# Two norms summed less their shift with one root operation, and softmax shares divided on ScalarE

## The reference, cut to what matters

```python
def layer_norm(x, g, b):
    mu = jnp.mean(x, -1, keepdims=True)
    var = jnp.mean(jnp.square(x - mu), -1, keepdims=True)
    return (x - mu) * lax.rsqrt(var + LN_EPS) * g + b

h = layer_norm(concatenate([meta, x]), emb_ln_g, emb_ln_b)        # "mean_e" in the kernel
for i in range(2):
    u = h @ w_in[i]                       # q, k, v, convolution input, two gates
    y_attn = sliding_window_attention(...) @ w_attn_proj[i]       # softmax with a sink
    y_conv = conformer_conv(...) @ w_conv_proj[i]                 # 31 taps, norm, silu
    mix = (sigmoid(ga) * y_attn + sigmoid(gc) * y_conv) @ w_out[i]
    h = layer_norm(ALPHA * h + mix, ln1_g[i], ln1_b[i])           # "n10", "n11"
    f = swiglu(h, ...) if i == 0 else moe_swiglu(h, ...)
    h = layer_norm(ALPHA * h + f, ln2_g[i], ln2_b[i])             # "n2", then the last norm

def sink_softmax(s, sink):
    m = jnp.maximum(jnp.max(s, -1, keepdims=True), sink)
    p = jnp.exp(s - m)
    return p / (jnp.sum(p, -1, keepdims=True) + jnp.exp(sink - m))
```

## Time and profile before

| what | value |
|---|---|
| median of 3 executions | 1641.17 us (1640.95 to 1641.51) |
| the profiled execution's own time | 1641.93 us |
| its span | 1640.1 us |
| PE busy | 1614.9 us, 98% of the span |
| PE's weight loads busy | 1472.9 us, 90% |
| DVE busy | 1240.9 us, 76% |
| ACT busy | 968.3 us, 59% |
| POOL busy | 304.4 us, 19% |
| mean granted TensorE clock, as a share of full speed | 0.999 |

### The profile page before, as it was taken

The page is one execution under the profiler, slowest core; times in us unless marked ns, Lnnn a source line. Parts: engine busy times, 40 slices in busy tenths (PEclk is TensorE's granted clock), DMA queues, the critical chain, the costliest instruction groups (busy, mean ns, idle before and its releaser), DMA issues.

```text
span 1640.1 us, 27535 instructions
## 1 busy us (share of the span) xinstructions
PE 1614.9 (98%) x11024; PEld 1472.9 (90%) x11024; DVE 1240.9 (76%) x1770; ACT 968.3 (59%) x1379; POOL 304.4 (19%) x301
## 2 busy tenths in 40 slices
PE   9999999999999999999999999999999999999997
PEld 8988888898888889989999999999988888888886
DVE  6565776666567656998975545899988898998897
ACT  6556674346657634555554433555568677776775
POOL 1230652123236302052300002131210000000000
PEclk9999999999999999999999999999999999999999
DMA  9732555563245546432435554534439898988983
GB/s 336 254 121 86 180 189 189 187 230 131 103 180 183 202 163 227 154 142 103 167 142 180 180 180 172 180 129 151 159 132 339 328 346 342 338 336 331 353 339 125
DMA packets 50740, 340.78 MB, mean 208 GB/s; under 512 B 5611, under 2 KB 7819, under 8 KB 11184
## 3 DMA queue, kind: packets, MB, share of 16 engines
q1 hardware_dynamic: 47920, 329.83, 54.9%
q0 software_dynamic: 2544, 9.12, 1.8%
q10 hardware_dynamic: 144, 0.01, 0.0%
HBM read 337.81 MB, written 1.13 MB: 207 GB/s over the span
## 4 chain that ended last, share of the span: by engine, by line
PE 86%; DVE 4%; issue 3%; ACT 3%; POOL 2%; DMA 1%; SPq 0%; POOLq 0%; DVEq 0%; ACTq 0%
PE bank L564 12%; PE bank L538 8%; PE bank L540 8%; PE bank L539 8%; PE bank L562 7%; PE bank L994 5%; PE bank L995 5%; PE bank L996 5%; PE bank L1027 2%; PE bank L1026 2%; PE bank L1025 2%; PE bank L691 2%; PE bank L693 2%; PE bank L692 2%; PE bank L444 1%
## 5 line engine op out<-in xcount | busy, mean ns | idle before, releaser
L1745 DVE TENSOR_TENSOR wl<-stg,wh 128x2048 fp32r<-128x2048 f32 x308 | 708.0, 2302 | 206.9 <-ACT wh L1239 204.2
L1239 ACT ACTIVATE wh<-stg 128x2048 fp32r<-128x2048 f32 x308 | 588.9, 1912 | 181.0 <-PE bank L996 81.3
L538 PE MATMUL bank<-xx,wh 128*128 128x272 f32 (+1 forms) x778 | 225.3, 290 | 0.0
L540 PE MATMUL bank<-xx,wl 128*128 128x272 f32 (+1 forms) x778 | 223.1, 287 | 0.0
L539 PE MATMUL bank<-xx,wh 128*128 128x272 f32 (+1 forms) x778 | 223.0, 287 | 0.0
L564 PE MATMUL bank<-xx,wh 128*128 128x512 f32 x448 | 159.7, 396 | 0.0
L564 PE MATMUL bank<-H,wh 128*128 128x512 f32 x434 | 151.3, 390 | 0.0
L994 PE MATMUL bank<-wh,GH 128*128 128x512 f32 (+3 forms) x400 | 147.5, 369 | 0.0
L539 PEld LDWEIGHTS bank<-xx,wh 128*128 128x128 f32 x778 | 147.4, 190 | 0.0
L538 PEld LDWEIGHTS bank<-xx,wh 128*128 128x128 f32 x778 | 146.4, 188 | 1.1 <-issue 0.7
L540 PEld LDWEIGHTS bank<-xx,wl 128*128 128x128 f32 x778 | 146.3, 188 | 0.0
(11 more groups left out here) (385 smaller groups left out, 3545.1 us busy)
## 6 DMA issues: line engine op xcount, KB each, us to landing
stg<-in_w SPq DMA_DIRECT2D x308, 1024.0 KB, 4.9
BT<-bias_scratch POOLq DMA_DIRECT2D x3, 1024.0 KB, 9.7
stg<-in_first SPq DMA_DIRECT2D x4, 512.0 KB, 6.1
stg<-in_w SPq DMA_DIRECT2D x4, 512.0 KB, 9.4
BT<-bias_scratch POOLq DMA_DIRECT2D x1, 2048.0 KB, 12.0
BB<-bias_scratch POOLq DMA_DIRECT2D x2, 1024.0 KB, 6.6
res<-in_x SPq DMA_DIRECT2D x1, 1024.0 KB, 8.8
BB<-bias_scratch POOLq DMA_DIRECT2D x2, 512.0 KB, 7.2
```

Source lines behind the costliest of these rows:

```text
L538: pe.matmul(out, wh, xh(kt), start=kt == 0, stop=False)
L540: ins = pe.matmul(out, wl, xh(kt), start=False, stop=kt == KT - 1)
L1239: act.activation(WH[u % NW][:, :], stg[place(u)][:, :], ACT.Copy).then_inc(*m.inc("w_high", u))
L1745: vec.tensor_tensor(WL[u % NW][:, :], stg[place(u)][:, :], WH[u % NW][:, :].bitcast(F32), ALU.subtract).then_inc(*m.inc("w_low_v", u))
```

## The change

Two things are changed. For the norms mean_e and n2 the sums, the root and the order of the last part get new forms (`..._ahead`); n10 and n11 keep theirs. In both mixing layers the shares move from POOL's program into ACT's.

- ACT makes 7 and 8 times the shift (`XC[3]` with a negative sign, `XC[5]`); POOL adds the former to the running sum.
- One tile ahead, DVE makes the last tile's known part less the shift (`less_shift`, `XC[6]`) and the first tile less the shift (`XC[2]`). At the last tile DVE first adds the product's part to it (`last_tile`), ahead of the sum into `RES`; PE and ACT take it from there.
- PE sums "less" (three terms less the shift), then the variance, then a plain mean, and then 4 instead of 11 products of ones.
- ACT squares the mean less shift and takes one Abs_reciprocal_sqrt where Ln and Exp were; its table is loaded at the place where the other's was.
- DVE makes the variance in one operation; the order over the tiles becomes normed, the low part of the tile before, the next centring.

```diff
+AHEAD_OF_SUMS = ("mean_e", "n2")
+            def last_sums_ahead(stage, name):
+                pe.matmul(PS[b][:, 0:T], ones, RS, start=True, stop=False)
+                pe.matmul(PS[v][:, 0:T], ones, SQ[:, 0, 0:T], start=True, stop=False)
+                w.wait_ge(*m.of("last_tile", name))
+                pe.matmul(PS[b][:, 0:T], ones, XC[:, KD - 2, :], start=False, stop=True)   # "less"
+                w.wait_ge(*m.of("shifted_sq", (name, KD - 1)))
+                pe.matmul(PS[v][:, 0:T], ones, SQ[:, KD - 1, 0:T], start=False, stop=True) # "var"
+                pe.matmul(PS[f][:, 0:T], ones, RS, start=True, stop=False)
+                pe.matmul(PS[f][:, 0:T], ones, XC[:, KD - 3, :], start=False, stop=False)
+                pe.matmul(PS[f][:, 0:T], ones, XC[:, KD - 2, :], start=False, stop=True)   # "mean"
+                keep_warm(4)
...
             def mix_layer(l, st):                                          # PE
-                        w.wait_ge(*m.of("shares", (tag, t)))
+                        w.wait_ge(*m.of("mixed_shares", (tag, t)))
...
+            def shifted_ahead(name, nt):                                   # ACT, last tile
+                    act.preload_act_table_set(ROOT)
+                    w.wait_ge(*m.of("last_tile", name))
+                    act.activation(SQ[:, KD - 1, :], XC[:, KD - 2, :], ACT.Square, scale=D ** -0.5)
+            def guess_ahead(name):
+                w.wait_ge(*m.of("group", (name, "less")))
+                act.activation(BC[:, :], bank((name, "less"))[:, 0:T], ACT.Square, scale=1.0 / D)
+                w.wait_ge(*m.of("var_out", name))
+                act.activation(BC[:, :], SQ[:, 2, :], ACT.Abs_reciprocal_sqrt)
+                sp.one_ahead()
...
                 def step(i):                                               # ACT, mixing layers
+                    d = i - 2
+                    if 0 <= d < len(jobs):
+                        L = a["L"][d % DEEP][0:nq, 1:1 + jobs[d]["nk"]]
+                        w.wait_ge(*m.of("recip", (tag, d)))
+                        act.activation(L, L, ACT.Copy, scale=a["z"][0:nq, d % (DEEP + 2), 4:5])
                     t = i - DEEP
...
+            def less_shift(name, scale):                                   # DVE
+                    ins = vec.tensor_tensor(XC[:, KD - 2, :], RES[:, KD - 1, :], SH, ALU.subtract)
+                vec.tensor_tensor(XC[:, 2, :], RES[:, 0, :], SH, ALU.subtract)
+            def last_tile(name, part, lo):
+                vec.tensor_tensor(XC[:, KD - 2, lo:T], XC[:, KD - 2, lo:T], part, ALU.add)
+            def shifted_norm_ahead(name, gname, l, low):
+                vec.scalar_tensor_tensor(v, var, LN_EPS, BC[:, :], ALU.add, ALU.subtract)  # var_out
+                first_tile()
+                w.wait_ge(*m.of("guess", name))
...
+                for kt in range(KD + 1):
+                    if kt < KD:
+                        w.wait_ge(*m.of("centred", (name, kt)))
+                        vec.scalar_tensor_tensor(SQ[:, kt, :], XC[:, kt if kt else 2, :], ...) # normed
+                    if kt == 0:
+                        w.wait_ge(*m.of("group", (name, "mean")))
+                        centre(1)
+                    if kt > 0:
+                        low(kt - 1)
+                    if 0 < kt < KD - 1:
+                        centre(kt + 1)
...
             def mix_layer(l):                                              # POOL
-                        w.wait_ge(*m.of("recip", (tag, i)))
-                        pool.tensor_scalar(L, L, z[0:j["nq"], 4:5], None, ALU.mult)
```

More of the change, by code:

```diff
@@ L773, in pump @@
                     if nt == 2:
-                        b, old = bank((name, "shift"), ("shift", name))
+                        b, old = bank((name, "shift"), ("shift_7" if name in AHEAD_OF_SUMS else "shift", name))
                         vacant(old)
@@ L798, in last_sums @@
                 keep_warm(11)
+            def last_sums_ahead(stage, name):
+                b, old = bank((name, "less"), ("centred", (name, 0)))
+                vacant(old)
+                w.wait_ge(*m.of("res_added", (name, "shifted")))
+                pe.matmul(PS[b][:, 0:T], ones, RS, start=True, stop=False)
+                v, old = bank((name, "var"), ("var_out", name))
+                vacant(old)
+                w.wait_ge(*m.of("sq_added", (name, KD - 2)))
+                pe.matmul(PS[v][:, 0:T], ones, SQ[:, 0, 0:T], start=True, stop=False)
+                w.wait_ge(*m.of("last_tile", name))
+                pe.matmul(PS[b][:, 0:T], ones, XC[:, KD - 2, :], start=False, stop=True).then_inc(*m.inc("group", (name, "less")))
+                w.wait_ge(*m.of("shifted_sq", (name, KD - 1)))
+                pe.matmul(PS[v][:, 0:T], ones, SQ[:, KD - 1, 0:T], start=False, stop=True).then_inc(*m.inc("group", (name, "var")))
+                f, old = bank((name, "mean"), ("centred", (name, KD - 1)))
+                if name == "n11":
+                    held.add(f)
+                vacant(old)
+                w.wait_ge(*m.of("shift_8", name))
+                pe.matmul(PS[f][:, 0:T], ones, RS, start=True, stop=False)
+                pe.matmul(PS[f][:, 0:T], ones, XC[:, KD - 3, :], start=False, stop=False)
+                pe.matmul(PS[f][:, 0:T], ones, XC[:, KD - 2, :], start=False, stop=True).then_inc(*m.inc("group", (name, "mean")))
+                keep_warm(4)
+            def last_sums(stage, name):
+                (last_sums_ahead if name in AHEAD_OF_SUMS else last_sums_plain)(stage, name)
             def mix_layer(l, st):
@@ L1431, in guess @@
                 sp.one_ahead()
+            def guess_ahead(name):
+                w.wait_ge(*m.of("group", (name, "less")))
+                act.activation(BC[:, :], bank((name, "less"))[:, 0:T], ACT.Square, scale=1.0 / D).then_inc(*m.inc("mean_sq", name))
+                w.wait_ge(*m.of("var_out", name))
+                act.activation(BC[:, :], SQ[:, 2, :], ACT.Abs_reciprocal_sqrt).then_inc(*m.inc("guess", name))
+                sp.one_ahead()
+            def guess(name):
+                (guess_ahead if name in AHEAD_OF_SUMS else guess_plain)(name)
             def split_norm(name, bname, l):
@@ L1475, in step @@
                 def step(i):
+                    d = i - 2
+                    if 0 <= d < len(jobs):
+                        nq = jobs[d]["nq"]
+                        L = a["L"][d % DEEP][0:nq, 1:1 + jobs[d]["nk"]]
+                        w.wait_ge(*m.of("recip", (tag, d)))
+                        act.activation(L, L, ACT.Copy, scale=a["z"][0:nq, d % (DEEP + 2), 4:5]).then_inc(*m.inc("mixed_shares", (tag, d)))
                     t = i - DEEP
@@ L1970, in shifted, with shifted_ahead, shifted_norm_plain @@
                     sp.hold()
-            def shifted_norm(name, gname, l, low):
+            def shifted_ahead(name, nt):
+                if nt == 3:
+                    w.wait_ge(*m.of("shift", name))
+                if nt == KD - 1:
+                    return
+                for kt in SHIFTED.get(nt, ()):
+                    w.wait_ge(*m.last("res"))
+                    vec.tensor_tensor(SQ[:, kt, :], RES[:, kt, :], SH, ALU.subtract).then_inc(*m.inc("shifted", (name, kt)))
+                if name == "n11" and nt == KD - 3:
+                    sp.hold()
+            def shifted(name, nt):
+                (shifted_ahead if name in AHEAD_OF_SUMS else shifted_plain)(name, nt)
+            def less_shift(name, scale):
+                if scale is None:
+                    ins = vec.tensor_tensor(XC[:, KD - 2, :], RES[:, KD - 1, :], SH, ALU.subtract)
+                else:
+                    ins = vec.scalar_tensor_tensor(XC[:, KD - 2, :], RES[:, KD - 1, :], scale, SH, ALU.mult, ALU.subtract)
+                ins.then_inc(*m.inc("less_shift", name))
+                vec.tensor_tensor(XC[:, 2, :], RES[:, 0, :], SH, ALU.subtract).then_inc(*m.inc("first_less", name))
+            def last_tile(name, part, lo):
+                w.wait_ge(*m.of("less_shift", name))
+                vec.tensor_tensor(XC[:, KD - 2, lo:T], XC[:, KD - 2, lo:T], part, ALU.add).then_inc(*m.inc("last_tile", name))
+            def shifted_norm_plain(name, gname, l, low):
                 d, v, t = SQ[:, 1, :], SQ[:, 2, :], SQ[:, 3, :]
@@ L2008, in shifted_norm, with centre, first_tile @@
                         low(kt - 1)
+            def shifted_norm_ahead(name, gname, l, low):
+                v, t = SQ[:, 2, :], SQ[:, 3, :]
+                less, mean, var = (bank((name, part))[:, 0:T] for part in ("less", "mean", "var"))
+                def centre(kt):
+                    vec.scalar_tensor_tensor(XC[:, kt, :], mean, -1.0 / D, RES[:, kt, 0:T], ALU.mult, ALU.add).then_inc(*m.inc("centred", (name, kt)))
+                def first_tile():
+                    w.wait_ge(*m.of("first_less", name))
+                    vec.scalar_tensor_tensor(XC[:, 2, :], less, -1.0 / D, XC[:, 2, :], ALU.mult, ALU.add).then_inc(*m.inc("centred", (name, 0)))
```

(33 more changed lines are left out.)

35 lines of the change are left out of this document (28 added, 7 removed).

## The result

The changed kernel took 1647.23 us (median of 7 runs, 1645.97 to 1648.38), the kernel before 1641.16 (7 runs, 1640.95 to 1641.51): a ratio of 1.0037, interval [1.0028, 1.0047]. The forecast was 1641.8 with a range to 1644.6; the time lies above it. The profiled execution took 1648.38 with a span of 1646.6.

The account below looks back on a forecast made before the run. The prediction took PE, 86% of the chain, as the bound, with DVE pacing the mixing layers. Its terms, -0.45 (mean_e, layer 0) and +1.1 (n2, layer 1), summed to +0.65: 1641.8 us, range 1637.7 to 1644.6.

Parts of the forecast that it names:

- the shares' price: Mixing layers: each share holds ACT's queue 0.42 or 0.32, delaying later work; priced at each layer's first values product.
- -0.45 for mean_e with layer 0: Net of mean_e's gain of -1.15, layer 0's later copies of turned shares, and part of POOL's 0.7 back.
- +1.1 for n2 with layer 1: Layer 1's first values product waits for ACT's copies, starting 0.9 to 1.4 late; n2's gain of -1.1 is gone.
- a slack of 1.34: Layer 0: the copy ends at 711.80, the first values product starts at 713.14; with new queue about 712.7.
- one reciprocal held up by 0.17: Layer 1, before the first values product: a pushed-back exponential holds up a reciprocal and what follows, some 0.17.
- the loop through ACT grows: Rival, 0.15: each pair of jobs loses its two shares anew round DVE and ACT; about +4.35, 1645.5.
- signs of being wrong: PE enters the dense FFN over 1 us early, or layers' DVE idle time vanishes and both lengthen over 2 us.
- The clock fell: Rival, 0.04: with 8 passes for 22 at the norm, clock falls to 1.2 GHz; a 2.4 us stretch costs +2.4.
- The norms' terms: mean_e and n2: sums -0.5, root -0.46, new tile order; second K tile -1.15 at mean_e, -1.1 at n2.
- That DVE would lose in the new order what it had gained: Over seven tiles of the norm DVE's cycle is 1.29 instead of 1.18; it leaves at the old time plus 0.2.
- POOL's waits: Layer 0: PE waited for POOL's shares 0.7 us, three times; part of it comes back with shares on ACT.
- the open question on the shared port: Mixing layers: whether POOL's shares hold DVE through the shared port; if so, moving them off POOL frees DVE.

Follow-up runs that it names:

- shares alone: The kernel before with the shares on ACT and all norms as before; 1645.64 us, ratio 1.0025.
- the norms alone: The changed kernel with the shares back on POOL, mean_e and n2 in their new forms; 1641.71 us, ratio 1.0004.
- the centring ahead: Changed kernel, shares behind both exponentials after weight copies and first in other pairs, DVE centring one tile further ahead in both norms; 1639.86 us, ratio 0.9992.
- no passes: Changed kernel with shares re-placed in ACT's queue and centring one tile further ahead, 0 instead of 4 products of ones in both norms; 1641.18 us, ratio 0.9998.
- each share twice in place: Changed kernel, each share at its changed place followed by one more copy of the same size; 1653.69 us, ratio 1.0074.
- the moved shares twice: Changed kernel, shares behind both exponentials after weight copies and first in other pairs, each followed by one more copy; 1641.83 us, ratio 1.0003.

## Why the prediction was wrong

- *The step that failed is the shares' price.* The sum had -0.45 for mean_e with layer 0 and +1.1 for n2 with layer 1; the table has -0.70 + 4.27 = +3.57 and -0.65 + 2.75 = +2.10. The price was worked out at one place of each layer, the first values product, as a delay handed once from ACT to PE. In layer 1 that place came out as forecast: the product waits 1.2 for the copied shares and starts about 1.4 later than before, counted from ahead of n2 (forecast 0.9 to 1.4); another 0.7 follows behind it. In layer 0 it was to be covered by a slack of 1.34; there the same product waits 0.7, then comes the wait of 1.6 for DVE's split, and then the clock. The exponentials were named as standing behind the shares, but the price counted only one reciprocal held up by 0.17. Measured, DVE waited for exponentials 2.9 and 3.6 us, eleven times, and these waits add up, since DVE has hardly any idle time there. The shares alone cost 3.29 and 1.76 of PE's time in the two layers, the clock included (4.2 us in the medians).
- *It was the rival "the loop through ACT grows"*, at 0.15 and 1645.5; the two runs at a mean clock of 0.999 took 1646.0 and 1646.1. Its mechanism held, and nearly its size: it counted four pairs in layer 1 and six in layer 0, half of the pairs there, 6.6 us in all; DVE's waits are 6.5, and PE lost 7.0 in the two layers, 1.6 of it by the clock. It did not say which pairs, and they are those behind a weight copy. The rows of before had the sign of it: the weight copy of 1.90 stands ahead of the narrow copy, and ACT's idle time of 13.8 us lies in other pairs of steps. ACT before, layer 0: it waits 1.90 for scores in the pair ahead of a copy and not at all in the pair behind it.

```profile
716.55 0.42 ACT L1491 ACTIVATE Lb<-Lb,zb 128x145 f32<-128x145 f32 x1 [1.90 <-DVE zb L2084]
...
717.78 1.89 ACT L1239 ACTIVATE wh<-stg 128x2048 fp32r<-128x2048 f32 x1
...
720.28 0.51 ACT L1491 ACTIVATE Lb<-Lb,zb 128x273 f32<-128x273 f32 x1
```

  The mean, ACT busy 6.56 of 10, hides that.
- *Of the signs of being wrong* the second came in half: both layers lengthened by over 2 us, but DVE's idle time in them grew, by its waits, instead of shrinking to nothing (from 668 to 760 it is busy 83.47 us, before 87.62).
- *The clock fell, at another place.* It was priced at the norm, at 0.04, where it did not fall with 4 products, and for a stretch of 2.4 us that no row gave. It fell in layer 0 where PE had come to wait, for 3.42 us, so a wait of 1.58 cost about 1.6 more.
- *The norms' terms* were right in kind: -0.87 for sums and root (forecast -0.96); -0.70 and -0.65 kept at the norms' exits, where -1.15 and -1.1 were forecast. The sum left out what PE needs to start after an idle time, 0.15 from the low part's end (657.03 + 0.49 = 657.52) to the product at 657.67. And it took the old starts from the chain: 657.64 where PE's timeline has 657.48, and 656.13 where it has 655.78, so the passes held the first product 0.39 and not 0.74 behind the high part's end. With 0.09, 0.15 and 0.16 taken off, 1.15 is 0.75; measured is 0.77.
- *That DVE would lose in the new order what it had gained* was right (0.37 and 0.41 later, forecast 0.2), and that the layers hand PE's lead back too: 0.79 and 0.90 with the norms alone. With the centring ahead all of -0.61 and -0.55 was kept.
- *POOL's waits* (0.7) and the open question on the shared port: the taps went from 500 to 495 ns, 1.5 us over all 240, and the long splits from 668 to 760 took 2284 and 2285 ns, so POOL had hardly held DVE. The Trainium skill, SBUF — State Buffer, "Who interferes with whom", has one or the other blocked by the order of issue; here the measurement says that it was POOL, as the earlier trace rows had shown. The same section of the Trainium skill says that ACT never waits on anyone; the shares' 509 and 401 ns, beside 512 and 408 for the exponentials of about the same shapes, fit that, but ACT's queue, not a port, was the question.

## What to carry to other kernels

A free engine is free at certain places of its queue. Before an operation moves there, ask what stands behind it in the same queue and who waits for that; the room is the idle time just before the next wait, not a mean over the stage. And where one engine paces a stage, a gain on another ahead of it is kept only if the pacing engine leaves the stage before earlier as well.

## What the runs showed of the hardware

The granted clock fell to 0.50 for 3.41 or 3.42 us at idle times of PE of 1.58 us (changed kernel, layer 0), 1.31 (shares alone, the same place) and 2.37 (no passes, n2); with each share twice in place it fell at idle times of 1.64 and 1.47 in layer 0, and in layer 1 some 2 us after one of 1.05. It stayed at 1.00 with 1.56 us idle from 820 to 824, after 0.65 at the norms, after 1.35 in layer 1 with the moved shares twice, and after 2.07 in layer 1 with each share twice in place. In the version without passes it did not fall at mean_e, after an idle time as long as that at n2:

```profile
654.33 0.36 PE L489 MATMUL bank<-xx,wh 128*128 128x272 f32 x1 [2.38 <-ACT xx L1499]
```

So the length of the one idle time does not tell these apart. What does is open: no run here varied the idle time alone.
